# Sixteen modulation weight units of a two-block transformer kernel: multiplied and added on VectorE instead of TensorE

## What is computed

```python
def modulate(h, shift, scale):
    return h * (1.0 + scale[:, None, :]) + shift[:, None, :]
# rows = silu(c) @ ada_w[layer] + ada_b[layer], cut into six pieces of 1024
# second input: the same with c_ctx
```

```python
        gates = jax.nn.sigmoid(gm.reshape(B, S, N_BRANCH, D))
        merged = gates[:, :, 0] * ua + gates[:, :, 1] * ub + gates[:, :, 2] * uc
        x = x + jnp.einsum('bsd,de->bse', merged, w_o[l])
```

## Time and profile before

| | us |
|---|---|
| median of 3 runs | 1142.0 |
| lowest and highest | 1141.15, 1144.45 |
| the profiled execution | 1138.87 |
| its span in the trace | 1137.1 |
| TensorE busy | 1086.0 |
| VectorE busy | 736.1 |
| ScalarE busy | 586.3 |
| GpSimd busy | 84.1 |

### The profile page before, as it was taken

How to read it: one execution, slowest core, us unless ns; L and a number is a source line. 1 busy time by engine, 2 the same in 40 slices (tenths; PEclk the granted TensorE clock), 3 DMA queues, 4 the chain that set the end, 5 groups by cost and what they waited for, 6 DMA issues and landing times.

```text
span 1137.1 us, 22032 instructions
## 1 busy us (share of the span) xinstructions
PE 1086.0 (96%) x9346; PEld 1019.8 (90%) x9346; DVE 736.1 (65%) x1094; ACT 586.3 (52%) x874; POOL 84.1 (7%) x93
## 2 busy tenths in 40 slices
PE   6999999999999989999898899999999999999997
PEld 5988778898889989999567899999989989999997
DVE  6467656654667686885575777774376767777643
ACT  5555655544445574722554664653454445656433
POOL 2000000100111360000011000000010010000000
PEclk9999999999999999999899999999999999999998
DMA  8556575786675584442577645556466457565631
GB/s 266 178 191 235 194 214 175 246 278 208 215 260 185 169 223 149 149 147 76 205 248 283 217 160 187 184 186 203 168 200 199 160 198 256 175 196 176 223 112 37
DMA packets 165774, 219.81 MB, mean 193 GB/s; under 512 B 4481, under 2 KB 146205, under 8 KB 165676
## 3 DMA queue, kind: packets, MB, share of 16 engines
q1 hardware_dynamic: 164442, 215.67, 58.0%
q0 software_dynamic: 832, 1.65, 0.7%
q10 hardware_dynamic: 402, 1.08, 0.4%
HBM read 217.27 MB, written 1.11 MB: 192 GB/s over the span
## 4 chain that ended last, share of the span: by engine, by line
PE 75%; DVE 14%; ACT 6%; issue 2%; DMA 2%; SPq 0%; POOL 0%; DVEq 0%; ACTq 0%
PE psG L491 18%; PE psG L493 18%; PE psG L492 18%; DVE wlo L1574 4%; PE psS L491 4%; PE psS L492 4%; PE psS L493 4%; PE psG L592 2%; ACT whi L1049 2%; DMA raw<-in_w_in_dram 2%; PE psY L866 1%; PE psY L617 1%; DVE Hlo L1639 1%; PE psS L696 1%; DVE vt L1630 1%
## 5 line engine op out<-in xcount | busy, mean ns | idle before, releaser
L1574 DVE TENSOR_TENSOR wlo<-raw,whi 128x1024 fp32r<-128x1024 f32 x311 | 376.3, 1246 | 154.3 <-ACT whi L1049 149.4
L491 PE MATMUL psG<-Hlo,whi 128*128 128x256 f32 x1520 | 435.3, 286 | 14.2 <-DVE wlo L1574 5.7
L493 PE MATMUL psG<-Hhi,whi 128*128 128x256 f32 x1520 | 428.2, 282 | 0.0
L492 PE MATMUL psG<-Hhi,wlo 128*128 128x256 f32 x1520 | 427.9, 281 | 0.0
L1049 ACT CAST whi<-raw 128x1024 fp32r<-128x1024 f32 x311 | 315.9, 1048 | 121.5 <-PE psS L493 68.3
L491 PEld LDWEIGHTS psG<-Hlo,whi 128*128 128x128 f32 x1520 | 286.4, 188 | 23.2 <-issue 10.1
L492 PEld LDWEIGHTS psG<-Hhi,wlo 128*128 128x128 f32 x1520 | 286.7, 189 | 0.1
L493 PEld LDWEIGHTS psG<-Hhi,whi 128*128 128x128 f32 x1520 | 286.3, 188 | 0.0
L491 PE MATMUL psS<-Glo,whi 128*128 128x256 f32 x352 | 99.4, 282 | 0.0
L492 PE MATMUL psS<-Ghi,wlo 128*128 128x256 f32 x352 | 99.1, 281 | 0.0
L493 PE MATMUL psS<-Ghi,whi 128*128 128x256 f32 x352 | 99.0, 281 | 0.0
(11 more groups left out here) (377 smaller groups left out, 1682.6 us busy)
## 6 DMA issues: line engine op xcount, KB each, us to landing
raw<-in_ada_w_dram SPq DMA_DIRECT2D x48, 1024.0 KB, 6.1
raw<-in_ffn_w_up_dram SPq DMA_DIRECT2D x44, 1024.0 KB, 5.1
raw<-in_w_in_dram SPq DMA_DIRECT2D x29, 1024.0 KB, 7.0
raw<-in_ev_w_in_dram SPq DMA_DIRECT2D x26, 1024.0 KB, 5.4
raw<-in_ffn_w_down_dram SPq DMA_DIRECT2D x22, 1024.0 KB, 4.9
raw<-in_od_w_in_dram SPq DMA_DIRECT2D x12, 1024.0 KB, 5.1
raw<-in_w_in_dram SPq DMA_DIRECT2D x9, 512.0 KB, 6.0
raw<-in_w_o_dram SPq DMA_DIRECT2D x4, 1024.0 KB, 8.1
```

The source lines that it names most:

```text
L491: mm(o, a_hi, b_lo, start=first, stop=False, skip_group_check=shared)
L492: mm(o, a_lo, b_hi, start=False, stop=False, skip_group_check=shared)
L493: return mm(o, a_hi, b_hi, start=False, stop=last, skip_group_check=shared)
L1574: V.tensor_tensor(ring_half(wlo, v, h - H0[v]), src, ring_half(whi, v, h - H0[v]).bitcast(F32), ALU.subtract).then_inc(lo_split, 1)
```

## The change

The ada units 8 to 23 (sections 2 to 5) become kind G. Each is multiplied and added on VectorE: for each of its two 128-row halves one instruction over 128 x 1024, weight times the condition's column, added to `arow` in place (`add_rows`). Only the latent condition's column is used; the context's modulation comes from sections 0 and 1. The first half of a section's first unit needs no addition. The slot of `raw` is free when VectorE is done (`row_added`). Once per section TensorE sums the row over the partitions with `ones` (`spread`, four matmuls side by side), ScalarE copies 256 columns back (`keep_spread`), and `sum_ada` goes on as before. GpSimd folds none of these four sections.  G units take no bank of `psG`. The two ada units of the `w_o` part move up behind branch c of rounds 0 and 1. The six other G units of the slots stay in their places: slots 8 to 13.

```diff
-            units.append(("A", f"ada{q // 24}", q % 4 * 2, q // 4 % 6 * D, D))
+            units.append(("G" if 8 <= q < 24 else "A", f"ada{q // 24}", q % 4 * 2, q // 4 % 6 * D, D))
...
-            if br != "c":
-                ada(f"gates{i}{br}", 1)
+            ada(f"gates{i}{br}", int(br != "c" or i < 2))
...
-        ada(f"wo{i}", int(i < 2))
...
-    banked = [int(k[0] != "D") for k in UNITS]
+    banked = [int(k[0] not in "DG") for k in UNITS]
...
                 if u >= RAW and UNITS[u - RAW][0] == "A":
-                    sp.wait_ge(ada_done, ADA.index(u - RAW) + 1)
+                    sp.wait_ge(ada_done, ON_PE.index(u - RAW) + 1)
+                elif u >= RAW and UNITS[u - RAW][0] == "G":
+                    sp.wait_ge(row_added, ON_DVE.index(u - RAW) + 1)
...
+            def spread(n):
+
+                pe.wait_ge(row_added, 4 * (n - 1))
+                pe.wait_ge(ada_kept, n)
+                for j in range(4):
+                    last = mm(psX[32 * j:32 * j + 32, 0:256], ones[:, 0:32], ada_row(n)[:, j * 256:(j + 1) * 256],
+                              start=True, stop=True)
+                last.then_inc(row_spread, 1)
...
-                    if br != "c":
-                        ada(f"gates{i}{br}")
-                if i == 0:
-                    sum_ada(3)
-                elif i == 1:
+                    if i < 3 and br == "a":
+                        if i == 0:
+                            pe.wait_ge(pT_kept, NT0)
+                        elif i == 2:
+                            pe.wait_ge(turned_kept, 8)
+                        spread(i + 2)
+                    elif i < 3 and br == "b":
+                        sum_ada(i + 2)
+                if i == 1:
                     pe.wait_ge(ada_kept, 4)
                     turn_tokens(1)
...
-                ada(f"wo{n}")
-            sum_ada(5)
+                if n == 0:
+                    spread(5)
+                elif n == 1:
+                    sum_ada(5)
...
+            def add_rows(place):
+
+                for u in SPAN[f"ada_{place}"]:
+                    i = ON_DVE.index(u)
+                    n, q = 2 + i // 4, i % 4
+                    r = ada_row(n)
+                    w = raw[:, u % RAW, :].rearrange("p (k n) -> p k n", k=2)
+                    dve.wait_ge(raw_landed[u % RAW], LANDED[u])
+                    if q == 0:
+                        dve.wait_ge(row_summed, n - 1)
+                    for k in range(2):
+                        c = cs[:, UNITS[u][2] + k, 0:1]
+                        if q == 0 and k == 0:
+                            ins = V.tensor_scalar(r, w[:, k, :], c, None, ALU.mult)
+                        else:
+                            ins = V.scalar_tensor_tensor(r, w[:, k, :], c, r, ALU.mult, ALU.add)
+                        if k == 0:
+                            step(ins)
+                    then(ins, row_added, i + 1)
...
+                if s >= 8:
+                    add_rows(f"slot{s}")
...
+                    if i < 3 and br == "c":
+                        keep_ada(i + 3)
                     dve.wait_ge(gate_e, n + 1)
...
-                    if b == 0:
-                        keep_ada((3, 4, 4, 5)[i])
+                    add_rows(f"gates{i}{br}")
...
-            for n in range(5):
+            for n in range(2):
                 fold_row(n)
             fold_squares("ctx")
-            fold_row(5)
             fold_squares("fin1")
```

More of the change, by code:

```diff
@@ L73, in ada @@
         for _ in range(n):
-            q = sum(unit[0] == "A" for unit in units)
-            units.append(("A", f"ada{q // 24}", q % 4 * 2, q // 4 % 6 * D, D))
+            q = sum(unit[0] in "AG" for unit in units)
+            units.append(("G" if 8 <= q < 24 else "A", f"ada{q // 24}", q % 4 * 2, q // 4 % 6 * D, D))
     first = {"qa": ("F", O_QA), "ka": ("F", O_KA), "va": ("T", O_VA), "qb": ("B", O_QB), "kvb": ("M", O_KB),
@@ L149, in build @@
            "ffn_down0": ffn_w_down_2[0], "ffn_down1": ffn_w_down_2[1], "ada0": ada_w_2[0], "ada1": ada_w_2[1]}
-    halves = {"C": 1, "U": 1, "V": 1, "A": 0}
+    halves = {"C": 1, "U": 1, "V": 1, "A": 0, "G": 0}
     NH = [halves.get(k[0], 2) for k in UNITS]
@@ L161, in build @@
     after = dict(zip(split_order, split_order[1:]))
-    ADA = [u for u in range(NU) if UNITS[u][0] == "A"]
+    ADA = [u for u in range(NU) if UNITS[u][0] in "AG"]
+    ON_PE = [u for u in ADA if UNITS[u][0] == "A"]
+    ON_DVE = [u for u in ADA if UNITS[u][0] == "G"]
     with ExitStack() as ctx:
@@ L307, in build @@
         sel8_set, row_folded, sq_folded = sem("sel8_set"), sem("row_folded"), sem("sq_folded")
+        row_added, row_spread = sem("row_added"), sem("row_spread")
         v_set, vhi_set = sem("v_set"), sem("vhi_set")
@@ L400, in build @@
         SLOT = [[SPAN[name][i] for name, i in units] for units in BESIDE]
-        KEEPS = [u for u in range(SLOT[-1][-1] + 1) if UNITS[u][0] not in "CA" and u not in
+        KEEPS = [u for u in range(SLOT[-1][-1] + 1) if UNITS[u][0] not in "CAG" and u not in
                  SPAN["ga"] + SPAN["gb"] + SPAN["gc"]]
@@ L409, in build @@
         GATES = SPAN["ga"] + SPAN["gb"] + SPAN["gc"]
-        SUM_AT = {5: 0, 10: 1, 13: 2}
+        SUM_AT = {5: 0, 10: 1}
+        SPREAD = range(2, 6)
+        FOLDS = [n for n in range(12) if n not in SPREAD]
         col = lambda ap: ap.rearrange("a (k p) -> (a k) p", p=P)
@@ L465, in _ @@
                                      ).then_inc(raw_landed[slot], 16)
-                elif kind in "DA":
+                elif kind in "DAG":
                     sp.dma_start(r.rearrange("p (k n) -> p k n", k=2),
@@ L586, in ada @@
                     pe.wait_ge(raw_landed[u % RAW], LANDED[u])
-                    if u == ADA[0]:
+                    if u == ON_PE[0]:
                         pe.wait_ge(c_silu, 1)
@@ L594, in ada @@
                     last.then_inc(ada_done, 1)
+            def spread(n):
[5 more added lines that the diff above has]
+                last.then_inc(row_spread, 1)
             def sum_ada(n):
-                pe.wait_ge(row_folded, n + 1)
+                if n in SPREAD:
+                    pe.wait_ge(row_ready, n + 1)
+                else:
+                    pe.wait_ge(row_folded, FOLDS.index(n) + 1)
                 if n:
@@ L747, in _ @@
                     project(u, Hhi, Hlo)
-                ada(f"slot{s}")
+                if s < 8:
+                    ada(f"slot{s}")
                 if s in SUM_AT:
@@ L1068, in keep_rows @@
                     n, q = ADA.index(u) // 4, ADA.index(u) % 4
-                    act.wait_ge(ada_done, ADA.index(u) + 1)
-                    if q == 0 and 2 <= n < 6:
-                        act.wait_ge(row_summed, n - 1)
+                    act.wait_ge(ada_done, ON_PE.index(u) + 1)
                     nc.scalar.copy(ada_row(n)[:, q * 256:(q + 1) * 256], bank(u)[:, 0:256]
@@ L1076, in keep_rows, with keep_spread @@
                         act.sem_inc(row_ready, 1)
+            def keep_spread(n):
+                act.wait_ge(row_spread, n - 1)
+                nc.scalar.copy(ada_row(n)[:, 0:256], psX[:, 0:256]).then_inc(row_ready, 1)
+                act.wait_ge(row_ready, n + 1)
             for rows, at, n in PAR_FIRST[1::2]:
@@ L1246, in _ @@
                         keep_first(u)
-                keep_rows(f"slot{s}")
+                if s < 8:
+                    keep_rows(f"slot{s}")
             ahead(SPAN["gm_a0"][0])
@@ L1268, in _ @@
                         high_of(2)
-                    if br != "c":
-                        keep_rows(f"gates{i}{br}")
+                    if i < 3 and br == "b":
+                        keep_spread(i + 2)
                 if i == 0:
@@ L1285, in _ @@
                 highs("ctx", mod[:, 0, 0:8, 1], Hhi, range(2 * n, 2 * n + 2))
-                keep_rows(f"wo{n}")
+                if n == 1:
+                    keep_spread(5)
             for g in range(4):
```

3 lines of the change are left out of this document (removed).

## The result

| | before | after |
|---|---|---|
| median, us | 1142.68 (1139.74 to 1144.45, 6 runs) | 1158.97 (1157.01 to 1163.77, 6 runs) |
| ratio, 95% interval | | 1.0144, 1.0124 to 1.0164 |
| the profiled execution | 1138.87 | 1157.27 |
| its span | 1137.1 | 1155.5 |

The account below looks back on a forecast made before the run. TensorE's matmuls and how early an ada unit returns its slot were taken to bound the gate part nearly together. Slots gain 6.1, the gate chain turns this into a 23.9 loss, `w_o` gains 2: +22 us, 1164; range 1151 to 1175.

Parts of the forecast that it names:

- the slots: Slots 8 to 13: a gain of 6.1 us, of it 4.2 from units 8 to 11; gm_a0's split ends at 195.7.
- the price of a G unit: On VectorE: 1.28 us per instruction over 1024; a unit takes 2.66 us, or 2.13 where it begins a section.
- the chain: Gate part: split, product, sum, G unit, next load and split in a loop; six stages take 79.8 us against 60.3.
- TensorE's wait: Gate-part stages: gm and up take TensorE 8.7 us, so it waits some 4 us in each, for `wlo`.
- the load: Gate-part chain: 6.02 us from issue to first rounding, a mean of five; 9.38 with round and split.
- rival (a): Gate part: the eight loads take 4.9 us, 1.1 less each, 9 us off, 1155; chance 0.10.
- The 4.4 us: Gate-part loads by the skill's formula: each of eight 1.6 us shorter, loss about 9 instead of 22; the forecast kept the rows.
- Rival (c): Gate part: loads of 6.7 add 5.4 us, a slow clock adds 2 x 3 behind gm_c2 and gm_c3; 1175, chance 0.12.
- the end: In the `w_o` part: two ada units (2.1 us) gone, a bank wait, spread and `keep_spread` wait come; gain 2 us.

Follow-up runs that it names:

- Five kernels: The changed kernel, the early release, the changed kernel with gate G units between split and product (1147.51 us), and the two kernels with added work.
- the early release: The changed kernel with each gate G unit moved ahead of the split of the next gate unit: 1133.38 us, ratio 0.9905 to before.
- the two kernels with added work: The changed kernel with four extra VectorE instructions at each gate-part G unit, ahead of it (1194.53 us) or behind the release (1172.89 us).
- the same move: The early release with slot 13's G unit also moved ahead of the split of gm_a0: 1131.46 us, ratio 0.9903 to before.

## Why the prediction was right, and where it was off

**Right: the slots.** The forecast had the split of gm_a0 end at 195.7; the next row on VectorE, slot 13's unit, begins at 195.81, against 201.77 before. Units 8 to 11 alone gave 3.0 us, as the forecast's 4.2 (with `spread`'s 0.5 off) would.

```profile
195.81 2.60 DVE L1664 SCALAR_TENSOR_TENSOR arow<-raw,cs,arow 128x1024 f32<-128x1024 f32 x2
```

**Right: the price of a G unit.** Worked out from 0.752 over 512 and 0.53 for the step from 512 to 1024 elements, 1.28 us; the groups by line and shape have

```profile
L1662 DVE TENSOR_SCALAR arow<-raw,cs x4: 753/754/755, 137.8 to 290.2; 128x1024 f32<-128x1024 f32 x4
...
L1664 DVE SCALAR_TENSOR_TENSOR arow<-raw,cs,arow x28: 1275/1285/1285, 138.6 to 337.0; 128x1024 f32<-128x1024 f32 x28
```

**Right: the chain.** It is in the profile as told, and in the six stages the splits of gate units end 11.8 to 13.4 us apart, where the forecast had 12 to 14. Five kernels that differ only in the place of the release or in work put beside it span 1133 to 1195 us. That it is the place and not the amount of work is shown within the stages by the early release and by the two kernels with added work. One link came out otherwise: at gm_b2 the chain runs over TensorE. It turns tokens behind `keep_ada` (from 276.16), then multiplies, at first with starts 0.21 us apart, and ScalarE rounds gm_b2 when that is done, at 285.90. The load was there by then, at most 5.57 us after its issue, so both ways were about equally long.

**Off: TensorE's wait.** The forecast had TensorE wait some 4 us for `wlo` in each stage. It idled in 12.7 of the 76.0 us from 225.05 to 301.06, 2.1 a stage. The other part of what a stage has over its 8.7 us went into matmuls at the lower clock and into small ones that the 8.7 leaves out, and several of the waits ended with ScalarE and not with `wlo` (below).

**Off: the load.** Six stages took 76.1 us, not 79.8. The term that was too long is the load, taken as the mean of five loads of before, 6.02 us. The eight took 5.53, 5.30, 5.63, 5.52, 5.26, 5.57, 5.44 and 5.44 us from issue to the first rounding, mean 5.46: 0.56 x 8 = 4.5 us too much in all. The 6.71 and 6.68 of the earlier trace rows didn't come back. So rival (a), short loads, was right in its direction by half of its 1.1 us a load. Why is open. Busy time and DMA share (the last but one number) ahead of two late gate loads of before, issued at 270.65 and 239.98:

```profile
266.00:270.60 4.60, 4.60 (x48) 3.88 (x46) 1.06 (x2) 0.60 (x1) 0.00 (x0) 1.00 0.50 200
...
236.00:239.90 3.90, 3.90 (x42) 3.19 (x40) 0.99 (x3) 0.60 (x1) 0.00 (x0) 1.00 0.71 263
```

Other loads were in flight ahead of both; in after the share ahead of the load at 229.15 is 0.00, and at most 0.02 ahead of six others. That fits shorter loads. But the eighth, issued at 241.74, had 0.80 ahead of it (239.0 to 241.7) and took 5.63, hardly more than the others, and of the two of before the one behind the busier stretch (0.71) was the shorter, 5.71 against 6.71, so the share alone doesn't order them, and no run isolated it. The 4.4 us that the Trainium skill's formula gives for 1 MiB ("DMA: Bandwidth & Descriptors", section "Anatomy of one DMA"; an estimate, from a fit to transfers that GpSimd issues) stays too short: the shortest of the eight was 5.26.

The sum by this term is 1161 - 4.5 = 1156.5, where 1157.27 was measured in the profiled execution. The median is 5.0 us under 1164 by three items: -4.5 for the load, +0.8 for all that follows below, and -1.4 because I had added 3.1 us from profiled execution to median, where after's lies 1.7 under its own. The +0.8 is itself what is left of errors of both signs, among them 2.3 us too little behind gm_c2 and 1.2 too much at the end (below), so that the sum meets the profiled execution within 1 us is in part luck.

**Missed or mis-priced: three waits on TensorE.** TensorE's starts in after:

```profile
236.99 0.39 PE L496 MATMUL psG<-Hlo,whi 128*128 128x256 f32 x1 [1.55 <-ACT gate L1288]
...
300.73 0.61 PE L621 MATMUL psX<-sel,arow 128*128 128x8 f32 x4 [2.65 <-ACT arow L1100]
301.20 0.36 PE L496 MATMUL psG<-Hlo,whi 128*128 128x256 f32 x1
...
333.28 0.39 PE L496 MATMUL psG<-Hlo,whi 128*128 128x256 f32 x1 [2.55 <-ACT gate L1288]
```

First, a G unit takes no bank, so the next gate unit takes the bank of the gate unit before it, and that is free only when ScalarE has made the gate from it, which stands in ScalarE's list behind the rounding of the next weight. Gate units wait for `gate`, where I had them wait for `wlo` (it is ready at about the same time). Second, `sum_ada` stands ahead of gm_c2 and waits for `keep_spread`, which stands behind the same rounding: gm_c2 begins at 301.20, not at the 300.0 that its split would allow. Third, the clock. Rival (c) had its drop right (0.57 from 226 to 230), and that it is hidden inside most stages: 72 matmuls of a branch took 10.3 instead of 8.8 us, but VectorE's chain runs past them. Behind gm_c2, where (c) had 3 us, it did cost:

```profile
302.00:305.00 3.00, 3.00 (x16) 3.00 (x16) 2.93 (x3) 1.04 (x1) 0.00 (x0) 0.51 0.02 7
```

The chain goes over these matmuls, and a branch of them takes 10.3 us once more, some 1.6 over full speed. Behind it VectorE's sum and its split of `merged` are slow (last section), and TensorE waits 1.38 us for the next split. From gm_c2's split to branch a's product of round 3 it was 20.8 us (301.06 to 321.83), forecast 18.5. Behind gm_c3 the clock was 1.00, and (c)'s other 3 us didn't come: the last product came 8.78 us after the split (334.10 to 342.88), forecast 8.4.

**Off: the end.** From the last product to the end of the span 3.2 us came back (21.6 to 18.4), forecast 2. Two ada units, 2.1 us, are gone from the `w_o` part; the other microsecond is less than a pair of profiles can tell there.

## What to carry to other kernels

When a step that frees a ring slot moves to another engine, write down what stands ahead of it in that engine's list, since the load behind the slot waits for all of it, and if that list itself waits for the load's product, a loop is closed whose length (here load 5.5, round and split 3.4, product and sum 1.6, release 2.7, in all 13.2 for a branch with a sum, measured 13.1 from 224.97 to 238.08) is the new stage time, whatever the engines' busy shares are. Put the release ahead of the work that waits for the next load: the same instructions in that order turned 1.4% slower into 0.9% faster. Then look where the freed step itself stands ahead of something that another engine waits for, as at gm_a0, since there the same move gave nothing that could be measured.

## What the runs showed of the hardware

Seven 1 MB loads that started with next to nothing in flight (DMA share 0.02 or less just ahead) took 5.26 to 5.57 us from their issue to the first use. In the kernel with the early release, where more is in flight (0.94 against 0.65 of the time), one issued at 234.92 took 9.20, and little of that shows: VectorE waited 1.54 us for its rounding, and TensorE idled 1.0 us from 246 to 248. A slow load costs little when it is issued early enough, and all of its length when it is the chain.

Two VectorE instructions beside GpSimd's took three times their time. GpSimd runs two additions over 128 x 1024 from 311.68 in after; VectorE's sum took 2.12 us and the cast behind it 1.40, where the same two take 0.69 and 0.43 a round later. The product ahead of them, which reads one of its two operands from `psG`, took its usual 0.69 at 311.68. It is the same in two other kernels: 2.15 and 1.41 us in before (from 291.25), 2.15 and 1.39 with the early release (from 286.70). No run isolated it:

```profile
311.68 4.09 POOL L2232 TENSOR_TENSOR tok<-tok 128x1024 f32<-128x1024 f32 x2 [180.61 <-ACT tok L1115]
```

```profile
312.51 2.12 DVE L1859 TENSOR_TENSOR merged<-merged,mt 128x512 f32<-128x512 f32 x1
314.66 1.40 DVE L1611 CAST Whi<-merged 128x512 fp32r<-128x512 f32 x1
```
